# A product-key expert layer: the scores x·U of tiles 1 to 3 formed densely and stored beside a copy of V

## The chip, the cores and the metric

One core of a Trainium2 chip runs the whole program. The metric is the device time of one execution in microseconds, the median of three runs.

## What is computed

One layer of a hybrid decoder for 512 prompt tokens and 8 sample tokens: two token mixers, then an expert layer (PEER) and a last norm. The change lies in the expert layer. The reference, cut to it:

```python
# x: (T, 1024) after an RMSNorm; 16384 experts, each one row of u_tab and one of v_tab (1024 values)
q = einsum('td,de->te', x, w_q).reshape(T, 8, 2, 128)
s = einsum('thpd,hpkd->thpk', q, keys)                # 8 heads, 2 axes, 128 keys
s_top, i_top = top_k(s, 16)                           # on each axis
cand = s_top[:, :, 0, :, None] + s_top[:, :, 1, None, :]      # 256 pairs
best, sel = top_k(cand, 16);  eidx = i0 * 128 + i1 of sel     # expert numbers
gate = softmax(best)
act  = gelu(einsum('td,thkd->thk', x, u_tab[eidx]))   # x . U of the chosen experts
y    = einsum('thk,thkd->td', gate * act, v_tab[eidx])
```

Every token uses 8 x 16 = 128 experts. h + y, normalised, is the output.

## The kernel before

Tokens are cut into tiles of 128 (0 to 3) and a tile of 8 samples. Before the experts run the phases of the mixers: `small_projection`, `stream` (the big projections, weights streamed by SP's queue and split into an upper and a lower part, so that each product is three matmuls, `mm3`), `convolve`, `delta_solve`, `delta_finish`, `retention`. In `convolve` and `delta_solve` a helper `Side` computes other projections beside: SP loads a weight of 512 KB (`load`), ACT rounds it (`round`, L646), POOL forms the lower part (L620), PE multiplies, ACT takes the product (L663).

The last phase is `experts`. A *unit* u is one head of one tile: 32 units and one for the samples. A *slot* n is one of the 16 experts of a unit: 4 x 128 slots, and 8 more in which the samples' 1024 experts lie spread over the partitions, 520 in all. `order` is the order of slots, p a place in it.

- POOL, for each slot (L1954): an indirect DMA that fetches for each of the 128 tokens the row of its expert from `peer_uv`, U and V side by side, 2048 floats, into one of RING = 7 buffers `uv_row`.
- DVE (`dot`, L2228): the product of the U half with x, summed into a column of `coef` (which lies in `ret_tables`).
- ACT (`row`, L2077 to L2087): GELU, times the gate, and a diagonal 128x128 matrix `spread` with it.
- PE (`add_row`, L1995): `spread` times the V half into PSUM, in float32, two halves of 512 columns, four matmul records in the trace. For the few slots in `by_vector` DVE adds coef times V instead (`add_vector`, L2236). A buffer is free when that is done, and POOL waits for it (`row_used`).
- In between, after slots given by the tables QUERIES_AT, TAKES_AT, SPLITS_AT and UPPERS_AT: the query projections (PE `queries`, with weights split by ACT L2057 and DVE L2162), scores, and on DVE the four steps of `retrieve` (top 16 of both axes, of the 256 pairs, expert numbers) and `normalise`. Tile by tile `add`, `root` and `scale` make the output.

DVE's work at the start of the phase: `make_x` and `lower_x` (L2279) give x, its upper and its lower part for the five tiles.

## Time and profile before

| | us |
|---|---|
| median of 3 runs | 2221.38 |
| lowest, highest | 2214.74, 2225.39 |
| span of the profiled execution | 2217.6 |
| first gather issued | 852.6 |
| last gather issued | 2193.3 |

The windows view cuts the span into stretches: for each, how long every engine was busy, the clock that TensorE was granted (1.00 is full), the share of time in which the 16 DMA engines were busy, and what they moved. Such a row tells what ends last in a stretch. The list of instructions in order of time then gives the price of a single piece of work and the distance from one to the next, and a view by line gives shortest, median and longest duration. A matmul's recorded duration covers its way through the array, so the distance between two starts is its price. The seven buffers hold what has been fetched and not yet used: as long as POOL waits for one to come free, DMA has work queued.

### The profile page before, as it was taken

How to read it: one execution, taken by the hardware profiler on the slowest of the kernel's cores; microseconds unless marked ns; L12 is line 12 of the kernel's file. 1: busy time of each engine (PE TensorE's matmuls, PEld its weight loads, DVE VectorE, ACT ScalarE, POOL GpSimd, SP SyncE). 2: the span in 40 equal slices, each digit the busy share in tenths (PEclk: the TensorE clock that was granted, in tenths of full speed). 3: DMA queues.
4: the chain of work that ended last, by engine and by line, in shares of the span. 5: the costliest groups of instructions: out<-in, count | busy, mean ns of one | idle time of the engine just before them, and what ended most of it. 6: DMA issues, size and time to landing. Idle time of an engine off the chain costs nothing.

```text
span 2217.6 us, 25834 instructions
## 1 busy us (share of the span) xinstructions
PE 1812.9 (82%) x8648; PEld 1169.7 (53%) x8648; DVE 1313.7 (59%) x2828; ACT 872.2 (39%) x2271; POOL 632.8 (29%) x553
## 2 busy tenths in 40 slices
PE   5989889979987888898887777777777777777776
PEld 4988889969966887565532222222323322222222
DVE  3127353353363537677766766767667866766764
ACT  4223322242244324444434444444443444444443
POOL 0002012100000002454434444444344443444442
PEclk8999899979998998999999999999999999999999
DMA  3313122335015329999999999999999999999997
GB/s 115 123 44 94 29 58 72 99 104 180 22 65 192 115 76 367 334 413 416 395 393 419 420 419 420 420 420 418 393 420 409 419 418 419 402 420 420 419 415 301
DMA packets 171933, 637.36 MB, mean 287 GB/s; under 512 B 12546, under 2 KB 97605, under 8 KB 104856
## 3 DMA queue, kind: packets, MB, share of 16 engines
q0 software_dynamic: 74880, 545.29, 60.0%
q1 hardware_dynamic: 96928, 90.50, 12.9%
q8 instruction: 66, 1.08, 0.2%
q14 instruction: 59, 0.48, 0.1%
HBM read 617.92 MB, written 17.93 MB: 287 GB/s over the span
## 4 chain that ended last, share of the span: by engine, by line
DMA 31%; PE 13%; DVE 8%; ACT 8%; issue 3%; DVEq 0%; ACTq 0%
DMA ex_uv_row<-in_peer_uv,ex_eidx 31%; PE ps L1995 10%; DVE ex_uv_row L2228 5%; ACT ex_spread L2087 2%; ACT L2077 1%; ACT ret_tables L2082 1%; ACT L2071 1%; PE ps L570 1%; PE ps L572 1%; PE ps L571 1%; ACT ret_tables L2077 1%; DMA ex_uv_row<-in_peer_uv,ex_eidx_s 1%; DVE ex_fin L2236 0%; DVE ex_w_lo L2162 0%; DVE ex_top_i L2190 0%
## 5 line engine op out<-in xcount | busy, mean ns | idle before, releaser
L1995 PE MATMUL ps<-ex_uv_row,ex_spread 128*128 128x512 f32 (+1 forms) x2016 | 964.0, 612 | 278.8 <-ACT ex_spread L2087 278.3
L1954 POOL DMA_INDIRECT ex_uv_row<-in_peer_uv,ex_eidx x512 | 561.2, 1096 | 1004.6 <-PE ps L1995 716.3
L2228 DVE CUSTOM_DVE_ANT_0 ex_uv_row<-ex_uv_row,x_ffn 128x1024 f32<-128x1024 f32 x512 | 624.2, 1225 | 360.4 <-DMA ex_uv_row<-in_peer_uv,ex_eidx 356.1
L1995 PEld LDWEIGHTS ps<-ex_uv_row,ex_spread 128*128 128x128 f32 (+1 forms) x2016 | 351.0, 189 | 851.5 <-issue 851.3
L2077 ACT ACTIVATE ret_tables<-ret_tables 128x1 f32<-128x1 f32 x520 | 104.9, 202 | 644.8 <-DVE ret_tables L2228 643.4
L2087 ACT ACTIVATE ex_spread<-square,ret_tables 128x128 f32<-128x128 f32 (+1 forms) x504 | 201.5, 400 | 16.5
L2082 ACT ACTIVATE ret_tables<-ret_tables 128x1 f32<-128x1 f32 x512 | 150.6, 294 | 17.1 <-ACT ret_tables L2077 0.2
L570 PE MATMUL ps<-proj_b_whi,x_lo 128*128 128x256 f32 (+1 forms) x320 | 91.1, 285 | 7.4 <-DVE proj_b_wlo L479 7.0
L570 PE MATMUL ps<-x_hi,ex_w_lo 128*128 128x260 f32 (+1 forms) x272 | 90.7, 334 | 6.1 <-DVE x_lo L2279 3.1
L572 PE MATMUL ps<-proj_b_whi,x_hi 128*128 128x256 f32 (+1 forms) x320 | 90.6, 283 | 0.0
L571 PE MATMUL ps<-proj_b_wlo,x_hi 128*128 128x256 f32 (+1 forms) x320 | 90.6, 283 | 0.0
L620 POOL TENSOR_TENSOR dp_w_lo<-dp_w_raw,dp_w_hi 128x1024 fp32r<-128x1024 f32 x14 | 33.9, 2427 | 171.5 <-ACT dp_w_hi L646 171.5
L571 PE MATMUL ps<-x_lo,ex_w_hi 128*128 128x260 f32 (+1 forms) x272 | 79.1, 291 | 0.0
L572 PE MATMUL ps<-x_hi,ex_w_hi 128*128 128x260 f32 (+1 forms) x272 | 79.0, 290 | 0.0
L634 PE MATMUL ps<-x_hi,dp_w_lo 128*128 128x260 f32 x224 | 66.3, 296 | 0.0
L636 PE MATMUL ps<-x_hi,dp_w_hi 128*128 128x260 f32 x224 | 63.8, 285 | 0.0
L635 PE MATMUL ps<-x_lo,dp_w_hi 128*128 128x260 f32 x224 | 63.7, 284 | 0.0
L620 POOL TENSOR_TENSOR cv_w_lo<-cv_w_raw,cv_w_hi 128x1024 fp32r<-128x1024 f32 x8 | 20.5, 2562 | 151.3 <-ACT cv_w_hi L646 151.3
L570 PEld LDWEIGHTS ps<-x_hi,ex_w_lo 128*128 128x128 f32 x272 | 54.2, 199 | 13.4 <-issue 6.8
L570 PEld LDWEIGHTS ps<-proj_b_whi,x_lo 128*128 128x128 f32 (+1 forms) x320 | 55.0, 172 | 9.5 <-issue 7.1
L570 PE MATMUL ps<-x_hi,proj_a_wlo 128*128 128x260 f32 x192 | 55.3, 288 | 5.0 <-DVE proj_a_wlo L479 5.0
L1078 ACT ACTIVATE Y<-ps 128x512 f32<-128x512 f32 x24 | 14.4, 599 | 110.1 <-PE ps L1031 110.1
(408 smaller groups left out, 3234.5 us busy)
## 6 DMA issues: line engine op xcount, KB each, us to landing
first_raw<-in_w_in SPq DMA_DIRECT2D x8, 1024.0 KB, 8.6
ex_uv_row<-in_peer_uv,ex_eidx POOLq DMA_INDIRECT x512
dp_w_raw<-in_w_in SPq DMA_DIRECT2D x14, 512.0 KB, 4.1
proj_a_raw<-in_w_in SPq DMA_DIRECT2D x4, 1024.0 KB, 5.2
cv_w_raw<-in_w_in SPq DMA_DIRECT2D x8, 512.0 KB
proj_b_raw<-in_w_in SPq DMA_DIRECT2D x4, 1024.0 KB, 5.4
S_sample<-in_state_ret SPq DMA_DIRECT2D x1, 4096.0 KB, 22.3
out_ret_s<-S_sample SPq DMA_DIRECT2D x4, 1024.0 KB, 4.4
```

The costliest lines, as they stand in the source:

```text
L570: pe.matmul(out, left(llo, c), right(rhi, c), start=(c == 0), stop=False)
L571: pe.matmul(out, left(lhi, c), right(rlo, c), start=False, stop=False)
L572: ins = pe.matmul(out, left(lhi, c), right(rhi, c), start=False, stop=(c == kc - 1))
L634: pe.matmul(out, self.w_lo[n % 2][:, c, :], self.hi[:, c, ts], start=(c == 0), stop=False)
L635: pe.matmul(out, self.w_hi[n % 2][:, c, :], self.lo[:, c, ts], start=False, stop=False)
L636: ins = pe.matmul(out, self.w_hi[n % 2][:, c, :], self.hi[:, c, ts], start=False, stop=(c == DC - 1))
L1954: pool.indirect_dma_start(uv_row[:, p % RING, :], None, a["peer_uv"][0], bass.IndirectOffsetOnAxis(ap=index_of(n), axis=0)).then_inc(row_l ...
L1995: ins = pe.matmul(k.pv[j % 2][0:r, c, :], spread[:, p % RING, 0:r], uv_row[:, p % RING, D + c * 512:D + (c + 1) * 512], start=first, stop= ...
L2077: fence(act, act.activation(c, c, ACT.Gelu), weighed, 2 * p + 1)
L2082: fence(act, act.activation(c, c, ACT.Copy, scale=gate_of(n)), weighed, 2 * p + 2)
L2087: act.activation(spread[:, p % RING, 0:what.shape[1]], what, ACT.Copy, scale=c).then_inc(spread_done, 1)
L2228: dve.tensor_tensor_reduce(u, u, x, 1.0, 0.0, ALU.mult, ALU.add, coef[:, n:n + 1]).then_inc(dotted, 1)
```

## The change

The table of experts has 16384 rows, in 128 blocks of 128. For tiles 1 to 3, 384 tokens, the change computes gelu(x U) for *all* experts by matmul, block by block, and stores 384 values per expert in a new DRAM tensor `value_rows`, one row per expert of 128 + 1024 + 256 floats: the values of tile 1, V, those of tiles 2 and 3. A gather of such a row for a token brings V and, next to it, the 128 values of its tile, of which the token's own is picked by the identity matrix.

- V is copied into `value_rows` by 16 DMAs of 1024 rows each, from DRAM to DRAM, that ACT issues: 4 in `convolve`, 12 in `delta_solve`.
- U comes transposed by blocks (`peer_ut`, laid out by the host as `peer_uv` is) and is loaded block by block, 512 KB each, like the query weights, through three buffers (DEEP = 3) for raw, upper and lower part. The order of blocks is `expert_blocks`: 16 blocks of queries among 128 of activities. ACT rounds (`upper`), DVE and POOL take turns at the lower part (`lower`), PE multiplies (`activities`, 24 matmuls of 384 columns), ACT applies GELU from PSUM (`activate`), SP stores 512 and 1024 bytes a row (`store`).
- Tile 0 keeps its paired rows, one slot for each block of activities, three blocks behind (LAG); all of them are added by DVE. The samples' 8 paired slots follow.
- Then the 384 slots of tiles 1 to 3 gather 1152 or 1280 floats a row into 11 buffers that lie where `uv_row` was. DVE makes the diagonal matrix itself (`picked`, one operation of 128 columns), every fourth slot it adds alone; ACT has no part in a slot.
- x of tiles 1 to 4 is kept in the upper half of q until its transposes are made; tile 0's in `x_first`.

The core of the diff:

```diff
+    def copy_values(self, act):
+        n = self.copies
+        part = slice(n * NE // COPIES, (n + 1) * NE // COPIES)
+        act.dma_start(self.value_rows[part, P:P + D], self.peer_uv[part, D:2 * D]).then_inc(self.values_copied, 16)
+        self.copies = n + 1
...
@@ convolve, ACT
                     act.activation(pre[:, c, 0:NP_TOK], taps[:, c % 2, :], ACT.Silu).then_inc(silu_done, 1)
+                    if c % 3 == 0:
+                        k.copy_values(act)
@@ delta_solve, ACT
                         act.activation(Y[:, n % 2, :, :], bank(4 + n % 2), ACT.Copy).then_inc(y_done, 1)
+                        if n % 2 == 0:
+                            k.copy_values(act)
@@ experts, SP
+                def load(i):
+                    kind, n = blocks[i]
+                    if i >= DEEP:
+                        lowered(sp, i - DEEP)
+                    src = columns(a["peer_wq"][0], n * P, P) if kind == "q" else a["peer_ut"][n]
+                    sp.dma_start(w_raw[i % DEEP][:, :, :], src).then_inc(w_loaded[i % DEEP], 16)
+                def store(b):
+                    sp.wait_ge(z_made, b + 1)
+                    to = k.value_rows[b * P:(b + 1) * P, :]
+                    sp.dma_start(to[:, 0:P], z_rows[:, b % DEEP, 0:P]).then_inc(z_stored[b % DEEP], 16)
+                    sp.dma_start(to[:, P + D:WROW], z_rows[:, b % DEEP, P:BT]).then_inc(z_stored[b % DEEP], 16)
@@ experts, POOL
-                    row_used(pool, p)
-                    pool.indirect_dma_start(uv_row[:, p % RING, :], None, a["peer_uv"][0],
-                                            bass.IndirectOffsetOnAxis(ap=index_of(n), axis=0)).then_inc(row_loaded[p % RING], 16)
+                for i, (kind, n) in enumerate(blocks):
+                    if kind == "z" and AHEAD <= n - LAG + AHEAD < PAIRS and n >= LAG:
+                        gather_pair(n - LAG + AHEAD)
+                    if 5 <= i + 2 < len(blocks) and not by_dve(i + 2):
+                        lower(pool, i + 2)
...
+                pool.wait_ge(k.values_copied, 16 * COPIES)
+                pool.wait_ge(vector_done, HK)
+                pool.wait_ge(v_done, PER_ROW)
+                for b in range(DEEP):
+                    pool.wait_ge(z_stored[b], 32 * len(range(b, NE // P, DEEP)))
+                for p in range(PAIRS, SLOTS):
+                    gather_value(p)
@@ experts, PE
+                def activities(i, b):
+                    lowered(pe, i)
+                    wait(pe, z_made, b - 1)
+                    mm3(pe, k.pb[b % 2][:, 0:BT], DC, lambda x, c: x[:, c, :], w_hi[i % DEEP], w_lo[i % DEEP],
+                        lambda x, c: x[:, c, P:NP_TOK], x_hi, x_lo).then_inc(z_mm, 1)
@@ experts, ACT
+                def activate(b):
+                    act.wait_ge(z_mm, b + 1)
+                    wait(act, z_stored[b % DEEP], 32 * (b // DEEP))
+                    act.activation(z_rows[:, b % DEEP, :], k.pb[b % 2][:, 0:BT], ACT.Gelu).then_inc(z_made, 1)
...
+                for i, (kind, n) in enumerate(blocks):
+                    if i and blocks[i - 1][0] == "z":
+                        activate(blocks[i - 1][1])
...
+                    if i and i + 2 < len(blocks):
+                        upper(i + 2)
+                    if kind == "z" and n >= LAG:
+                        row(n - LAG)
@@ experts, DVE
+                def picked(p):
+                    n, m = order[p], p - PAIRS
+                    z = value_slot(p)[2]
+                    dve.wait_ge(gated, place[n // TOPK] + 1)
+                    dve.wait_ge(value_loaded[m % VALUES], 16 * (m // VALUES + 1))
+                    if p in by_vector:
+                        own.fence(dve.tensor_tensor_reduce(z, z, k.eye, gate_of(n), 0.0, ALU.mult, ALU.add, coef[:, n:n + 1]))
+                    else:
+                        wait(dve, v_done, on_tensor[p] - SPREADS + 1)
+                        dve.scalar_tensor_tensor(spread[:, on_tensor[p] % SPREADS, :], z, gate_of(n), k.eye,
+                                                 ALU.mult, ALU.mult).then_inc(diagonal, 1)
```

How it moves instructions. On ACT in `delta_solve`, before (Y is the Y of the solve, dp_result a product of the side work):

```order
L1078 ACTIVATE Y<-ps 128x512
L646 ACTIVATE dp_w_hi<-dp_w_raw 128x1024
L663 ACTIVATE dp_result<-ps 128x260
L1078 ACTIVATE Y<-ps 128x512
L663 ACTIVATE dp_result<-ps 128x260
```

and after:

```order
L1111 ACTIVATE Y<-ps 128x512
L177 DMA value_rows<-in_peer_uv 1024x1024
L656 ACTIVATE dp_w_hi<-dp_w_raw 128x1024
L673 ACTIVATE dp_result<-ps 128x260
L1111 ACTIVATE Y<-ps 128x512
L673 ACTIVATE dp_result<-ps 128x260
```

Behind every second Y stands the issue of a copy, ahead of the rounding. On DVE among tile 0's slots, before (L2228 is a dot, two rows each; L2208 to L2216 the last step of a retrieval):

```order
L2228 ISA ex_uv_row,ret_tables<-ex_uv_row,x_ffn 128x1024
L2228 ISA ret_tables 128x1
L2208 TENSOR_SCALAR ex_pick<-ex_sel 128x16
L2209 TENSOR_SCALAR ex_pick<-ex_sel 128x16
L2211 TENSOR_TENSOR ex_hot<-ex_pick,square 128x512
L2213 TENSOR_TENSOR ex_hot<-ex_hot,ex_top_f 128x512
L2215 TENSOR_REDUCE ex_res<-ex_hot 128x32
L2216 SCALAR_TENSOR_TENSOR ex_eidx<-ex_res 128x16
L2228 ISA ex_uv_row,ret_tables<-ex_uv_row,x_ffn 128x1024
L2228 ISA ret_tables 128x1
```

and after (L2367 dot, L2379 addition of V, L1929 lower part):

```order
L2367 ISA ex_uv_row,ret_tables<-ex_uv_row,x_first 128x1024
L2367 ISA ret_tables 128x1
L2379 SCALAR_TENSOR_TENSOR ex_fin<-ex_uv_row,ret_tables,ex_fin 128x1024
L1929 TENSOR_TENSOR ex_w_lo<-ex_w_raw,ex_w_hi 128x1024
L2367 ISA ex_uv_row,ret_tables<-ex_uv_row,x_first 128x1024
L2367 ISA ret_tables 128x1
L2379 SCALAR_TENSOR_TENSOR ex_fin<-ex_uv_row,ret_tables,ex_fin 128x1024
```

Each dot is now followed by the addition, and every second block by a lower part. On POOL, the whole phase before:

```order
L1954 DMA ex_uv_row<-in_peer_uv,ex_eidx 128x2048 x384
L1954 DMA ex_uv_row<-in_peer_uv,ex_eidx_s 128x2048 x8
L1954 DMA ex_uv_row<-in_peer_uv,ex_eidx 128x2048 x128
```

and after, the last rows of it:

```order
L2040 DMA ex_uv_row<-in_peer_uv,ex_eidx 128x2048 x2
L1929 TENSOR_TENSOR ex_w_lo<-ex_w_raw,ex_w_hi 128x1024
L2040 DMA ex_uv_row<-in_peer_uv,ex_eidx 128x2048
L2040 DMA ex_uv_row<-in_peer_uv,ex_eidx_s 128x2048 x8
L2051 DMA ex_uv_row<-value_rows,ex_eidx 128x1152 x256
L2051 DMA ex_uv_row<-value_rows,ex_eidx 128x1280 x128
```

Subtractions stand among the pairs' gathers, and the value gathers behind them all.

## Rows read from the trace of the kernel before

**Rows 1.** Windows: length, busy us (count) per engine, PE clock, DMA share, GB/s.

```profile
500.00:610.00 110.00, 108.31 (x921) 102.66 (x921) 40.00 (x47) 28.14 (x47) 1.42 (x2) 1.00 0.31 98
1100.00:1860.00 760.00, 584.48 (x1360) 230.48 (x1360) 528.02 (x1275) 333.43 (x984) 315.83 (x298) 0.99 1.01 415
```

**Rows 2.** The page: its span, and the chain that ended last.

```profile
span 2217.6 us, 25834 instructions
...
DMA 31%; PE 13%; DVE 8%; ACT 8%; issue 3%; DVEq 0%; ACTq 0%
```

**Rows 3.** By line, POOL's gathers: ns min/median/max, first and last start.

```profile
L1954 POOL DMA_INDIRECT ex_uv_row<-in_peer_uv,ex_eidx x512: 932/937/1988, 852.6 to 2193.3; - x171
```

**Rows 4.** In order of time: start, length, engine, line, [idle before it].

```profile
378.46 0.60 ACT L1078 ACTIVATE Y<-ps 128x512 f32<-128x512 f32 x1 [4.68 <-PE ps L1031]
...
380.69 0.43 SPq L600 DMA_DIRECT2D dp_w_raw<-in_w_in  x1
...
389.60 0.60 ACT L1078 ACTIVATE Y<-ps 128x512 f32<-128x512 f32 x1 [4.68 <-PE ps L1031]
...
390.09 1.05 ACT L646 ACTIVATE dp_w_hi<-dp_w_raw 128x1024 fp32r<-128x1024 f32 x1
...
395.17 0.60 ACT L1078 ACTIVATE Y<-ps 128x512 f32<-128x512 f32 x1 [3.75 <-PE ps L1031]
...
828.82 4.67 SPq L1905 DMA_DIRECT2D wq_raw<-in_peer_wq  x1
```

**Rows 5.** DMA issues, 300-432 and 1200-1700 us: KB each, us to landing.

```profile
dp_w_raw<-in_w_in SPq DMA_DIRECT2D x10, 512.0 KB, 4.1
...
out_y_p<-ex_fin SPq DMA_DIRECT2D x2, 512.0 KB, 8.2
```

**Rows 6.** In order of time, PE: the first and the last of 147 matmuls.

```profile
739.80 0.28 PE L571 MATMUL ps<-x_lo,branches_whi 128*128 128x260 f32 x1
...
757.22 0.28 PE L570 MATMUL ps<-x_hi,branches_wlo 128*128 128x260 f32 x1
```

**Rows 7.** The page's DMA queues: packets, MB, share of 16 engines over the span.

```profile
q0 software_dynamic: 74880, 545.29, 60.0%
q1 hardware_dynamic: 96928, 90.50, 12.9%
```

**Rows 8.** By line, DVE: dot, addition of V, lower part; ns min/median/max.

```profile
L2228 DVE CUSTOM_DVE_ANT_0 ex_uv_row<-ex_uv_row,x_ffn x512: 1205/1225/1301, 859.0 to 2206.1; 128x1024 f32<-128x1024 f32 x171
...
L2236 DVE SCALAR_TENSOR_TENSOR ex_fin<-ex_uv_row,ret_tables,ex_fin x16: 1278/1284/1285, 865.9 to 2209.3; 128x1024 f32<-128x1024 f32 x16
...
L2162 DVE TENSOR_TENSOR ex_w_lo<-wq_raw,ex_w_hi x8: 1215/1220/1221, 834.1 to 1101.6; 128x1024 fp32r<-128x1024 f32 x8
```

**Rows 9.** In order of time, DVE: last x_lo, two dots, the last dot.

```profile
856.11 1.36 DVE L2279 TENSOR_TENSOR x_lo<-ps,x_hi 128x1024 fp32r<-128x1024 f32 x2 [0.52 <-ACT x_hi L2110]
...
1516.22 1.22 DVE L2228 CUSTOM_DVE_ANT_0 ex_uv_row<-ex_uv_row,x_ffn 128x1024 f32<-128x1024 f32 x1
...
1517.40 1.23 DVE L2228 CUSTOM_DVE_ANT_0 ex_uv_row<-ex_uv_row,x_ffn 128x1024 f32<-128x1024 f32 x1
...
2206.13 1.23 DVE L2228 CUSTOM_DVE_ANT_0 ex_uv_row<-ex_uv_row,x_ffn 128x1024 f32<-128x1024 f32 x1 [1.25 <-DMA ex_uv_row<-in_peer_uv,ex_eidx]
```

**Rows 10.** In order of time, convolution: taps alone, and beside POOL's subtraction.

```profile
168.35 2.33 DVE L894 SCALAR_TENSOR_TENSOR conv_taps<-pre,vecs,conv_taps 128x512 f32<-128x512 f32 x3
...
179.25 4.35 DVE L894 SCALAR_TENSOR_TENSOR conv_taps<-pre,vecs,conv_taps 128x512 f32<-128x512 f32 x3
...
179.79 2.46 POOL L620 TENSOR_TENSOR cv_w_lo<-cv_w_raw,cv_w_hi 128x1024 fp32r<-128x1024 f32 x1 [3.64 <-ACT cv_w_hi L646]
```

**Rows 11.** In the chain of waits: twelve matmul records of three rows on PE.

```profile
943.51 5.15 PE ps L1995 x12
```

**Rows 12.** The page's group of the gathers: busy us, mean ns | idle before.

```profile
L1954 POOL DMA_INDIRECT ex_uv_row<-in_peer_uv,ex_eidx x512 | 561.2, 1096 | 1004.6 <-PE ps L1995 716.3
```

**Rows 13.** In order of time, POOL: a gather's issue, [idle before it].

```profile
854.00 0.94 POOL L1954 DMA_INDIRECT ex_uv_row<-in_peer_uv,ex_eidx  x1 [0.30 <-issue]
```

518 lines of the change are left out of this document (310 added, 208 removed).

## The prediction

> **What bounds the kernel now.** I read the windows by stage first, because the share of a whole span mixes stages. From 1100 to 1860 us the DMA share is 1.01 at 415 GB/s, while PE is busy 584 of 760 us, DVE 528 and ACT 333 [rows 1]. That is the stage that gathers one paired row (U and V, 8 KB for each of 128 partitions, 1.0486 MB) for each of 520 slots. The chain of waits agrees: its largest piece by far is the gather, 31% [rows 2]. 1.0486 MB at 415 GB/s is 2.53 us, and 520 gathers run from 852.6 to 2193.3 us [rows 3]. Before the gathers, from 500 to 610 us for example, DMA moves 98 GB/s and PE is busy 108 of 110 us [rows 1]: there the matmuls bound, and DMA is three quarters idle. The change attacks the bytes of the first stage and spends DMA in the second and matmuls in the first. So the question is what a "block" of the new dense stage costs, and what a slot of the new value stage costs.
>
> **What is there before the experts.** 16 copies of 4.19 MB, HBM to HBM, are issued by ACT: four in the convolution and twelve in the delta solve, one behind every second Y, whose period is 11.1 us (378.46 to 389.60) [rows 4]. No such copy is in the trace. Bounds: each byte once through the engines at 415 GB/s is 10.1 us a copy; each byte twice is 20.2. By the first all is done by about 432 us, by the second by about 560. Who can suffer: the side load behind which ACT waits. It is issued at 380.69, wanted at 390.09, lands in 4.1 us; beside saturated gathers a load or store of this size takes 8.2 [rows 4, 5], still under 9.4. And ACT itself: SP's fifth issue in a row took 4.67 us where a single one takes 0.4 [rows 4], so a queue with about four such transfers open holds its issuer. At 20.2 us a copy the twelfth finds 12 x (1 - 11.1/20.2) = 5.4 open; some 3 issues would be held for up to 9 us. ACT has 3.75 us of idle before each Y. Cost 0 to 27 us; I take 5, nearer to none because every named wait has slack.
>
> **The dense stage.** I count one unit: 16 blocks of activities and 2 of queries; there are eight (the last without queries, -11 us).
> - PE: 147 matmuls of 260 columns start between 739.80 and 757.22 us, 0.1193 us apart at full granted clock [rows 6]. 384 columns: 0.176 if all of it scales, 0.171 if only columns at 2.4 GHz are added. 16 x 24 x 0.171 = 65.7, queries 2 x 48 x 0.1193 = 11.5, scores about 0.6: **78 us** (80 by the upper price).
> - DMA: from the two queues of the page, 284 ns for 7282 bytes and 47 ns for 934 bytes an engine (share x span x 16 / packets), I work out 12.3 ns a packet plus 0.0373 ns a byte [rows 7]. 16 pairs x 2.53 = 40.4, 16 U blocks (8 packets of 4 KB an engine) x 1.32 = 21.1, two query weights 4.0, stores of z in 512 and 1024 byte runs 16 x 0.65 = 10.5: **76 us**.
> - DVE: dots follow each other at 1.18 us (1516.22 to 1517.40), the addition of V is 1.28: 16 x 2.46 = 39.4. Half of the lower parts, 9 x 1.22 = 11.0 [rows 8, 9]. Retrieval: 528.0 us busy less 304 dots of 1.30 is 132 us over 19 units, 6.9, with its gaps about 8; normalise 0.4. Sum 59.
> - On top, POOL takes the other 9 lower parts. What that does to DVE is in the convolution: three taps take 2.33 us alone and 4.35 with one POOL subtraction beside them, so DVE stands 2.0 us for each [rows 10]. 9 x 2.02 = 18. DVE with what it is made to wait: **77 us**. A gather's own issue stretches from 0.94 to at most 1.99 and does not stretch the dots (1301 ns at most) [rows 3, 8].
> - The three raw buffers: load 8.2 us under load, ACT's upper part 1.05, lower part 1.22 or 2.46 (on POOL), and about 2.5 behind the dot and the addition that stand ahead in DVE's order: 13 to 14.2 us for three blocks [rows 4, 5, 8, 10], 4.3 to 4.7 a block, 78 to 85 us a unit.
> ACT has about 2.4 us of work in 4.3. Four limits within ten per cent, coupled by in-order waits, do not reach the largest of them: I take 84 us a unit, the buffers' figure. 8 x 84 - 11 = **661 us**; ends 613 (PE alone) and 750 (95 a unit: POOL's 2.37 and its wait both added, and no overlap).
> The stage starts when the last x_lo is made. That was at 857.5 [rows 9]; a retrieval of 8 us that stood ahead now stands behind, so 852 is taken. End: 852 + 661 = 1513.
>
> **Between the stages.** Value rows lie where the pairs lay, so POOL waits for the last pair to be used. After the last block DVE has 11 dots, 5 additions, a retrieval and a normalise: 13 + 6.4 + 8.5 = 28, then ACT and PE 5: 33 us, in which six gathers (15 us) are hidden and DMA falls idle. 1546, first value row 3 us later.
>
> **The value stage.** 256 rows of 4608 and 128 of 5120 bytes a partition. By bytes at 415 GB/s 1.42 and 1.58 us; with the cost of a packet worked out above 1.48 and 1.63. The middle: 256 x 1.45 + 128 x 1.61 = **577 us** (566 to 588). Beside it: PE, 294 of 384 rows; a row of four matmul records costs 1.72 (5.15 for three) [rows 11], and 12 x 1.72 + 0.6 = 21.2 in a unit of 16 against DMA's 23.2. DVE about 19. POOL 0.94 for an issue, 1.10 on average as it waits for DVE, and 0.30 to the next: 1.40 a slot against 1.45 [rows 3, 12, 13]. All hidden, but POOL by 3% only.
> The end is as it was: the last dot starts at 2206.13, 11.5 us before the end of the span [rows 2, 9].
>
> **Sum.** 1546 + 3 + 577 + 11.5 + 5 (copies) = 2143 of span. The profiled execution has a span of 2217.6, and the median of the runs, 2221.4, lies 3.8 above it (runs from 2214.7 to 2225.4); the profile gives no time of its own outside the span. Forecast 2143 + 3 = **2146 us**, 3.4% faster. The gather stage gives 1353 up for 661 + 36 + 577.
>
> **Rivals.**
> A, slower: the raw buffers decide the dense stage and their loads land later than 8.2 us, since not only gathers but gathers and z stores stand ahead of them. Every microsecond of landing costs 144 / 3 = 48 us, because PE, DVE and the gathers all follow the blocks. It outweighs the gain from a landing of 9.8 us; at 11 the time is 2146 + 134 = 2280. For it: DMA is 76 of 84 us busy there, a share at which the only landings measured are already double. Against: the 8.2 was measured at a share of 1.0.
> B, copies at 20 us and ACT held at every issue from the first: 12 x 9.1 = 109 us, 2250. Against: four transfers fit before SP is held, and a third of that is nearer, 2175. The Trainium skill ("DMA: Bandwidth & Descriptors", Latency and other measured facts) gives 214 GB/s for a good copy between HBM tensors; by that a copy takes 19.6 us, an estimate, and the slow side of my bounds would hold: all copies done only by about 550 us, and 2175 rather than 2146. No row here shows a copy between HBM tensors of this size, so none confirms it.
> C, faster: DVE and POOL find each other's gaps and PE alone bounds at 78 us a unit: 613, and value rows cost bytes only, 566: 2087.
> D, POOL bounds the value stage: its wait for DVE grows since DVE's short operations come oftener; 1.55 a slot is 595, and with a unit at 90 us (+48) the time is 2212, no change.
> That the gather does not shrink is no rival: the shapes 128x1152 and 128x1280 stand in the program.
>
> **How the numbers follow.** Chance of the forecast and what lies around it (2105 to 2200) 0.56; C 0.14; the mild form of B is inside the first; D 0.10; A 0.14; strong B 0.06. A measurement of this kernel can tell 0.5%, 11 us, from no change. Faster by more (under 2210): 0.56 + 0.14 + 0.03 = 0.73; within 0.5%: 0.09; slower: 0.18. The range that leaves out 2 in 10: from C's 2087 to 2240, where the dense stage costs its upper end of 750 (2235).
>
> **What would show it.** Right: windows of the dense stage with DMA near 0.9, PE near 0.93 of the time, 4.6 us a block; lower parts on POOL of about 2.5 us and DVE additions that stand beside them; value stage at DMA 1.0, 1.45 to 1.6 us a gather; stages up to 825 us unmoved. Wrong: ACT's upper part waiting for the load (A); ACT's copy issues of many microseconds and later Y's (B); POOL without idle time among the value gathers (D). The working is wrong as a whole if a block takes over 5.1 us, for then nothing is gained.

## The result, and the profile after

The changed kernel takes 2280.2 us (median of 4 runs, 2274.0 to 2285.4), the kernel before 2218.3: a ratio of 1.027, 95% interval 1.024 to 1.030. It is slower by 2.7%, where 2146 us and 3.4% faster had been forecast, and outside the range of 2087 to 2240. The profiled execution has a span of 2283.6 us against 2217.6 [rows 2].

These are lines of the page of the changed kernel: the span, PE's granted clock and the DMA share in 40 slices of 57 us, the queues with packets, MB and share of the 16 engines, and the chain that ended last.

```profile
span 2283.6 us, 29645 instructions
...
PEclk9997788887799989999999999999999999999999
DMA  3316415988350154269999999999989999999997
...
q0 software_dynamic: 74880, 377.52, 42.0%
q1 hardware_dynamic: 152224, 182.80, 23.4%
q10 hardware_dynamic: 16640, 67.11, 8.6%
...
PE 24%; DMA 14%; DVE 11%; issue 5%; POOL 2%; ACT 1%; SPq 0%; DVEq 0%; another core or an unknown queue 0%; ACTq 0%; POOLq 0%
```

q0 and q1 answer to [rows 7]: the gathers move 377.5 MB where they moved 545.3. q10 is new, the sixteen copies of V. In the chain PE now has the largest share and no longer DMA as in [rows 2]; by line its largest piece is still a gather, that of the value rows, with 11% where the paired rows had 31%. In the slices from the fourth to the tenth the DMA share is up to 9 and PE's granted clock is down to 0.7; that is the convolution and the delta solve, where the copies run.

Two windows answer to [rows 1]: the dense stage from its first activity to its last, and the gathers of values (length, busy us and count for PE, PEld, DVE, ACT and POOL, clock, DMA share, GB/s).

```profile
998.90:1648.50 649.60, 627.19 (x3740) 621.57 (x3738) 572.85 (x762) 293.46 (x595) 363.89 (x196) 0.99 0.96 357
...
1677.80:2258.50 580.70, 521.41 (x1230) 220.27 (x1231) 420.11 (x1332) 21.40 (x62) 400.30 (x384) 1.00 1.01 406
```

In the first PE is busy 627.2 of 649.6 us. The forecast counted from the last x_lo, which is made by 977.0 here: on that measure the stage takes 671.5 us where 661 were forecast. The second has a DMA share of 1.01 at 406 GB/s, like the gathers of before.

By line, this is the row of the activities z on ACT (ns min/median/max, first and last start):

```profile
L2202 ACT ACTIVATE ex_z_rows<-ps x128: 491/493/496, 998.9 to 1648.5; 128x384 f32<-128x384 f32 x128
```

and of the gathers of values:

```profile
L2051 POOL DMA_INDIRECT ex_uv_row<-value_rows,ex_eidx x384: 935/941/2003, 1677.8 to 2258.5; - x192
```

128 activities from 998.9 to 1648.5 us. 384 gathers start between 1677.8 and 2258.5: 1.512 us each, where 1.45 and 1.61 (1.503 in the mean) were forecast. So the two new stages take nearly what was said. But both lie some 130 us late, since the dense stage can begin only when the mixers have ended. The place of the delay is in ACT's waits (us in total, times, longest):

```profile
ACT ex_w_hi L2189 <- DMA ex_w_raw<-in_peer_ut: 91.6, 46, 6.8
ACT cv_w_hi L656 <- DMA cv_w_raw<-in_w_in: 74.9, 6, 17.4
ACT dp_w_hi L656 <- DMA dp_w_raw<-in_w_in: 73.1, 5, 15.1
```

The last two are new in size (in the kernel before it is 10.6 us for cv_w_hi and nothing for dp_w_hi): 148 us in which ACT, whose work is in order, stands before the upper part of a side weight and waits for its load. In the convolution it looks like this, on ACT (start, length, engine, line, [idle before it and what ended it]):

```profile
174.41 0.61 ACTq L177 DMA_DIRECT2D value_rows<-in_peer_uv  x1
...
194.39 1.06 ACT L656 ACTIVATE cv_w_hi<-cv_w_raw 128x1024 fp32r<-128x1024 f32 x1 [16.42 <-DMA cv_w_raw<-in_w_in]
```

SP's load between them:

```profile
176.02 0.98 SPq L610 DMA_DIRECT2D cv_w_raw<-in_w_in  x1
```

ACT issues a copy at 174.41, SP a side load at 176.02, and ACT waits 16.42 us for it, until 194.39. In the kernel before the same load and the same use stood so, on SP:

```profile
174.38 0.44 SPq L600 DMA_DIRECT2D cv_w_raw<-in_w_in  x1
```

and ACT's use of it:

```profile
178.65 1.06 ACT L646 ACTIVATE cv_w_hi<-cv_w_raw 128x1024 fp32r<-128x1024 f32 x1 [2.31 <-DMA cv_w_raw<-in_w_in]
```

The load landed in 4.3 us, and ACT waited 2.31 us for it even then. This row was not among those the prediction rests on: in the convolution a side load had no slack at all, before any copy.

In the delta solve, a stretch of ACT in order of time that answers to [rows 4]:

```profile
395.55 0.50 ACTq L177 DMA_DIRECT2D value_rows<-in_peer_uv  x1
...
406.67 0.50 ACTq L177 DMA_DIRECT2D value_rows<-in_peer_uv  x1
...
421.64 1.06 ACT L656 ACTIVATE dp_w_hi<-dp_w_raw 128x1024 fp32r<-128x1024 f32 x1 [14.38 <-DMA dp_w_raw<-in_w_in]
```

and SP's load:

```profile
397.92 0.64 SPq L610 DMA_DIRECT2D dp_w_raw<-in_w_in  x1
```

The load that took 4.1 us [rows 5] takes 23.7, and the Y behind it waits. This is so for every second load of the solve: the one issued in between, at 388.17, finds the copies nearly done and is used at 396.18 without a wait.

### The profile page after: what moved, and what is told of

It reads as the page before. It is cut to its first block, busy times and chain, and to the rows that moved or that the text cites. A ratio compares the mean times of both kernels' runs of the same rounds, so it can differ in the third digit from the quotient of the medians.

```text
span 2283.6 us, 29645 instructions
## 1 busy us (share of the span) xinstructions
PE 1960.3 (86%) x10912; PEld 1591.0 (70%) x10912; DVE 1397.7 (61%) x2791; ACT 611.5 (27%) x1217; POOL 845.6 (37%) x625
## 4 chain that ended last, share of the span: by engine, by line
PE 24%; DMA 14%; DVE 11%; issue 5%; POOL 2%; ACT 1%; SPq 0%; DVEq 0%; another core or an unknown queue 0%; ACTq 0%; POOLq 0%
DMA ex_uv_row<-value_rows,ex_eidx 11%; PE ps L2129 9%; PE ps L580 5%; PE ps L582 5%; PE ps L581 5%; DVE ex_fin L2379 4%; DMA ex_w_raw<-in_peer_ut 3%; POOL ex_uv_row L2051 2%; DVE ex_uv_row L2367 2%; DVE ex_w_lo L1929 1%; ACT ex_w_hi L2189 0%; DVE ex_q_s L2392 0%; DMA ex_w_raw<-in_peer_wq 0%; DVE ex_hot L2349 0%; DVE ex_top_i L2326 0%
## 5 line engine op out<-in xcount | busy, mean ns | idle before, releaser
L2129 PE MATMUL ps<-ex_uv_row,ex_q_s 128*128 128x512 f32 (+1 forms) x1208 | 544.5, 600 | 76.2 <-DVE ex_q_s L2392 46.3
L2129 PEld LDWEIGHTS ps<-ex_uv_row,ex_q_s 128*128 128x128 f32 (+1 forms) x1208 | 216.9, 187 | 387.7 <-issue 357.1
L2051 POOL DMA_INDIRECT ex_uv_row<-value_rows,ex_eidx x384 | 401.2, 1045 | 195.3 <-issue 95.1
L580 PE MATMUL ps<-x_hi,ex_w_lo 128*128 128x384 f32 (+2 forms) x1296 | 428.0, 330 | 21.1 <-DVE ex_w_lo L1929 15.2
L582 PE MATMUL ps<-x_hi,ex_w_hi 128*128 128x384 f32 (+2 forms) x1296 | 425.0, 328 | 0.0
L581 PE MATMUL ps<-x_lo,ex_w_hi 128*128 128x384 f32 (+2 forms) x1296 | 424.6, 328 | 0.0
L2379 DVE SCALAR_TENSOR_TENSOR ex_fin<-ex_uv_row,ret_tables,ex_fin 128x1024 f32<-128x1024 f32 x218 | 364.2, 1671 | 15.0 <-ACT ret_tables L2219 14.9
L1929 POOL TENSOR_TENSOR ex_w_lo<-ex_w_raw,ex_w_hi 128x1024 fp32r<-128x1024 f32 x72 | 187.9, 2610 | 407.8 <-ACT ex_w_hi L2189 407.2
L581 PEld LDWEIGHTS ps<-x_lo,ex_w_hi 128*128 128x128 f32 x1296 | 245.8, 190 | 0.0
L582 PEld LDWEIGHTS ps<-x_hi,ex_w_hi 128*128 128x128 f32 x1296 | 245.6, 190 | 0.0
L2040 POOL DMA_INDIRECT ex_uv_row<-in_peer_uv,ex_eidx x128 | 183.6, 1434 | 116.3 <-DVE ex_fin L2379 98.7
L2367 DVE CUSTOM_DVE_ANT_0 ex_uv_row<-ex_uv_row,x_first 128x1024 f32<-128x1024 f32 x128 | 175.3, 1370 | 1.0
L1929 DVE TENSOR_TENSOR ex_w_lo<-ex_w_raw,ex_w_hi 128x1024 fp32r<-128x1024 f32 x72 | 88.5, 1229 | 68.0 <-ACT ex_w_hi L2189 49.0
L630 POOL TENSOR_TENSOR cv_w_lo<-cv_w_raw,cv_w_hi 128x1024 fp32r<-128x1024 f32 x8 | 20.2, 2534 | 205.2 <-ACT cv_w_hi L656 205.2
```

The lines of the kernel that those rows point to most:

```text
L580: pe.matmul(out, left(llo, c), right(rhi, c), start=(c == 0), stop=False)
L581: pe.matmul(out, left(lhi, c), right(rlo, c), start=False, stop=False)
L582: ins = pe.matmul(out, left(lhi, c), right(rhi, c), start=False, stop=(c == kc - 1))
L1929: eng.tensor_tensor(w_lo[b][:, :, :], w_raw[b][:, :, :], w_hi[b][:, :, :].bitcast(F32), ALU.subtract).then_inc(split_v if by_dve(i) else s ...
L2040: pool.indirect_dma_start(uv_row[:, p % RING, :], None, a["peer_uv"][0], bass.IndirectOffsetOnAxis(ap=index, axis=0)).then_inc(pair_loaded ...
L2051: pool.indirect_dma_start(value_slot(p)[0], None, k.value_rows, bass.IndirectOffsetOnAxis(ap=eidx[:, u, n % TOPK:n % TOPK + 1], axis=0), e ...
```

## Experiments: did the copies cost it, and where

All runs compare with the kernel before on the same chip (2215.3 to 2217.3 us in the four groups). The theory after the first look, called T: the copies cost nothing by themselves; side loads land late behind them and hold ACT, Y and PE. Rivals: another part of the change delays the mixers (R), or the new stages pay for the copies too (W).

**Without copies.** The value rows are gathered from the paired tensor with unchanged shapes, so that what is added is not V.

```
-                    if c % 3 == 0:
-                        k.copy_values(act)
...
-                        if n % 2 == 0:
-                            k.copy_values(act)
...
-                    pool.indirect_dma_start(value_slot(p)[0], None, k.value_rows,
+                    pool.indirect_dma_start(value_slot(p)[0], None, k.peer_uv,
...
-                pool.wait_ge(k.values_copied, 16 * COPIES)
```

> The changed kernel without the sixteen copies of V; its value rows are gathered with the same shapes from the paired tensor instead (the values taken are therefore not V, only the bytes and the instructions are the same). Theory T: the copies cost nothing in themselves, but the side loads (512 KB in packets of 512 bytes) land behind them, ACT waits for them and with it Y and PE; all 128 to 131 us by which the dense stage began later come from that. Then the stages up to 825 us stand where they stood before, the first dense block at about 853, and the time is 2280 - 129 = 2151 (2143 to 2160). Rival R: the mixers are late for another reason that the change brings (its code, its placement of buffers, a lower clock by itself): then 2250 or more. A third, W: the dense stage or the value stage also pays for the copies: under 2140.

2155.6 us, ratio 0.972 (0.969 to 0.975). T's number was 2151. The activities, by line:

```profile
L2196 ACT ACTIVATE ex_z_rows<-ps x128: 472/493/497, 868.4 to 1522.2; 128x384 f32<-128x384 f32 x128
```

The first is at 868.4, 130.5 us earlier than with copies, and the stage takes 653.8 us against 649.6. All of the loss, then, lies ahead of the dense stage, and none of it in the new stages. R and W fall.

**The copies alone, in the kernel before.**

```
+                    if c % 3 == 0:
+                        k.copy_values(act)
...
+                        if n % 2 == 0:
+                            k.copy_values(act)
```

> The kernel before with the same sixteen copies at the same places and nothing else of the change; nobody reads what they write. By T the mixers are delayed as in the changed kernel and the rest is as before: 2218 + 129 = 2347 (2335 to 2360). By R, where the delay came with something else of the change, 2218 to 2245. Where gathers of the paired rows hid part of it: between the two, which the first gather's start would show (T: 852.6 + 130 = 983).

2355.6 us, ratio 1.064 (1.062 to 1.065): 140 us more, 9 above the expected 2347. ACT's waits are those of the changed kernel, to a microsecond:

```profile
ACT cv_w_hi L655 <- DMA cv_w_raw<-in_w_in: 74.7, 6, 17.7
ACT dp_w_hi L655 <- DMA dp_w_raw<-in_w_in: 73.6, 5, 15.2
```

Its gathers, by line:

```profile
L1969 POOL DMA_INDIRECT ex_uv_row<-in_peer_uv,ex_eidx x512: 932/938/1977, 984.1 to 2323.8; - x171
```

The first gather starts at 984.1, where [rows 3] have 852.6: 131.5 us. In the profiled execution that is the whole cost: its span is 2348.1 us, 130.5 more than 2217.6. It was the fastest of the four, at 2350.0 us, so the rest of the 140 is the spread of the runs. Nothing of the dense stage is in this kernel, so the copies and their places are a sufficient cause.

## Experiments: how a copy holds up a load on another queue

A copy of 4.19 MB takes 12.3 us of all sixteen engines: q10's 8.6% of 2283.6 us over 16 copies, or 189 ns for each of its 64 packets of 4 KB an engine. That is near the fast side of the prediction's bounds, 10.1 to 20.2, and still the loads took 18 to 24 us. T1: packets of the two queues take turns, and a load of 64 short packets an engine (512 KB in runs of 512 bytes) and the store issued just ahead of it (8 more) wait for a long one at each turn. T2: a load is served when the copies issued before it have moved.

**Shorter packets for the copies.**

```
+        quarters = lambda x: x.rearrange("n (a b) -> a n b", b=D // 4)
-        act.dma_start(self.value_rows[part, P:P + D], self.peer_uv[part, D:2 * D])...
+        act.dma_start(quarters(self.value_rows[part, P:P + D]), quarters(self.peer_uv[part, D:2 * D]))...
```

> The changed kernel with each copy's rows of 4096 bytes cut into four packets of 1024 bytes, the same bytes, issues and places. Two theories on why a side load lands after 15 to 24 us beside a copy. T1, turns by packet: each of the load's 64 packets an engine waits for about one packet of the copy (189 ns for 4096 bytes on the page of the changed kernel, 64 x (189 + 47) = 15 us); with packets of 1024 bytes, some 55 to 65 ns, it is 64 x 110 ns = 7 us and 2 of latency, which is inside the 9.4 us of slack: the time is 2150 to 2175. T2, order: a load issued behind a copy lands when the copies issued before it have moved their bytes, whatever their packets: no change, 2270 to 2290, or worse if short packets move fewer bytes in the same time.

2644.8 us, ratio 1.195 (1.192 to 1.199), which neither theory had. On ACT:

```profile
174.81 1.23 ACTq L178 DMA_DIRECT2D value_rows<-in_peer_uv  x1
...
186.38 1.06 ACT L657 ACTIVATE cv_w_hi<-cv_w_raw 128x1024 fp32r<-128x1024 f32 x1 [8.00 <-DMA cv_w_raw<-in_w_in]
186.57 33.62 ACTq L178 DMA_DIRECT2D value_rows<-in_peer_uv  x1
...
220.31 1.06 ACT L657 ACTIVATE cv_w_hi<-cv_w_raw 128x1024 fp32r<-128x1024 f32 x1 [31.29 <-issue]
```

A window in which nothing but the second copy moves:

```profile
204.00:218.00 14.00, 0.00 (x0) 0.00 (x0) 0.00 (x0) 0.00 (x0) 0.00 (x0) 0.50 0.27 97
```

With four times the packets a copy of 4.19 MB becomes an issue of 32 to 40 us on ACT's queue in 14 of the 16 places (the first of the convolution took 1.23 us, the first of the solve 0.64), and the engines are nearly three quarters idle while it trickles at 97 GB/s. That is a new cost, not the one in question. The side load issued at 176.42 lands at 186.38, in 10 us, while the copy ahead of it still moves; T2 says no such thing, T1 does. But the engines are not full beside this load, so its 10 us are no measure of the turns.

**Long packets for the loads.** The side loads read a tensor in which a partition's 4096 bytes lie together, so that what is computed from them is not the layer's.

```
-                         columns(self.w, side_column(self.tiles[n]), P)).then_inc(self.loaded[n % 2], 16)
+                         self.k.wide[self.tiles[n]]).then_inc(self.loaded[n % 2], 16)
```

> The changed kernel, copies as they are, with one size changed: the side loads of 512 KB come from a tensor in which each partition's 4096 bytes lie together, so a load has 8 packets of 4 KB an engine in place of 64 of 512 bytes (the side weights are therefore other numbers, and all that is made of them is wrong; bytes, instructions and waits are the same). T1, one packet of the copy for each packet of the load: 8 x (189 + 189) = 3 us and 2 of latency, where the load of 64 packets took 17.8 us beside a copy (64 x 278 ns): ACT's waits for side loads in the convolution and the delta solve go from 148 us to under 20 and the time is 2150 to 2175. T3, the two queues share bytes, or a load waits for the copy ahead of it: a load of the same bytes lands when it did, 2265 to 2285.

2225.8 us, ratio 1.004 (1.003 to 1.006): 54 us come back, between the two expectations. The first side load behind a copy lands in 12.5 us (176.44 to 188.97), the one in the delta solve that is issued at 333.09 in 12.5 too. T1 gave 5 (7 with the store's packets counted), T2 the end of the copy, at about 188 and 345: here T2 looks right. It is not: by the trace's records of single packets the copy issued at 174.83 ended at 192.2, with 725 of its 1024 packets moved when the load had landed. The solve's side loads span 166.5 us against 148.4.

**Half the copy at the old places.** Sixteen copies of 2.1 MB by ACT, the other half of the bytes from SP at the ends of three projections.

```
-COPIES = 16
+COPIES = 32
+COPIES_IN = {"proj_a": 4, "proj_b": 7, "branches": 0, "w_out": 5}
...
+                for _ in range(COPIES_IN[name]):
+                    k.copy_values(sp)
```

> The changed kernel with each of ACT's sixteen copies at its old place and half its size, 2.1 MB; the other 16 x 2.1 MB go from SP at the ends of three projections (4, 7, 5), where they cost nothing by the kernel with all copies behind loads. How a side load of 512 KB, issued by SP 1 to 2 us behind a copy of ACT, is held up. T2, order at the engines: it lands when the copy issued before it has moved (4.19 MB take 12.3 us by the page, so 14.5 + 4 = 18 us in the changed kernel, 17.8 measured; with wide packets 12.5 measured, though they were 8 in place of 64). Half the copy is 6.2 us: the load lands in 10 to 12 us. It costs then (10.5 - 4.1) / (17.8 - 4.1) of 59 us in the convolution, 27, and 2 us for each of some ten loads in the delta solve: 2150 + 47 = 2197 (2175 to 2215). T1, turns packet by packet: the copy still has 128 packets an engine for the load's 64, so every turn is taken as before, the load lands in 17 to 18 us, and only the second copy in the delta solve's 24 us falls away: convolution as late as in the changed kernel, 2225 to 2275.

2175.8 us, ratio 0.982 (0.980 to 0.984), at the lower edge of what T2 was given. On ACT:

```profile
174.98 0.61 ACTq L178 DMA_DIRECT2D value_rows<-in_peer_uv  x1
...
187.34 1.06 ACT L659 ACTIVATE cv_w_hi<-cv_w_raw 128x1024 fp32r<-128x1024 f32 x1 [8.81 <-DMA cv_w_raw<-in_w_in]
```

and SP's load:

```profile
176.59 0.84 SPq L613 DMA_DIRECT2D cv_w_raw<-in_w_in  x1
```

The load of 176.59 lands at 187.34, in 10.75 us. The first side load of the delta solve is at 283.1 us, against 255.6 in a kernel whose convolution has no copies (below): 27.5, where 27 was expected. The 20 us expected in the delta solve did not come: its loads land after 8.5 to 10.8 us, ACT waits 0.3 to 1.5 us each, and they span 150.5 us. There the 9.4 us of [rows 4] and ACT's own idle time do hold. But the reckoning of T1 in this expectation was wrong: 2.1 MB are 32 packets an engine, not 128, so the copy is used up before the load's turns are, and both theories give about 11 us.

**The same halves, issued behind the load.**

```
-                        if n % 2 == 0:
+                        if n % 2 == 1:
```

> The same with one place changed: in the delta solve the twelve copies of 2.1 MB stand behind the odd Ys in place of the even ones, so that ACT issues each 2 to 4 us behind a side load in place of 1 to 2 us ahead of it. T2: what is issued later does not hold a load up, the copy has moved within 6.2 us of an interval of 11.1, and the delta solve is as without copies (149 us from its first side load to its last), while the convolution costs what it costs in the kernel with half copies: 20 us less than that, 2177 (2160 to 2195). If the two kernels take the same time, the place in the order is not what counts and the solve pays for the bytes in flight as such.

2179.8 us, ratio 0.985 (0.982 to 0.987), not the 20 us less that were expected, for the reason just told: half copies had cost the solve nothing at the old place either. ACT's upper parts there have no wait at all now, where they had up to 1.5 us.

**Double copies.** The test that tells the theories apart is a copy that outlives the load.

```
-COPIES = 16
+COPIES = 8
...
-                    if c % 3 == 0:
+                    if c % 6 == 0:
...
-                        if n % 2 == 0:
+                        if n % 4 == 0:
```

> The changed kernel with eight copies of 8.4 MB in place of sixteen of 4.19 MB, each at the place of every second one. The kernel with half copies was reckoned wrongly: a copy of 2.1 MB has 32 packets of 4 KB an engine, not 128 (512 rows over 16 engines), fewer than the load's 64, so that by turns too the load outlives the copy and lands after 2 + 6.2 + what is left of its own, as measured: it did not tell T1 from T2. A copy longer than the load does. First side load behind a copy in the convolution, issued 1.6 us behind it. T1, turns: a load and the store ahead of it have 72 packets an engine, the copy 128, so 72 x (189 + 47) ns = 17 us and 2 of latency, 18 to 20 us, no more than the 17.8 beside 4.19 MB. T2, the copy ahead first: 2 + 24.6 + 4.3 - 1.6 = 29 us. The time tells less, since half of the loads have no new copy ahead: 2240 to 2290 by T1, 2270 to 2320 by T2.

> The same with side loads of long packets, 8 of 4 KB an engine and 8 of the store ahead of them (the side weights are other numbers, and what is made of them is wrong). T1, one packet of the copy for each: 16 x 189 + 2 of their own + 2 of latency = 7 us, and not the 11 to 12.5 measured beside 4.19 MB. T2: 2 + 24.6 + 0.5 - 1.6 = 25 us. T3, a fixed backlog: the engines have taken in some 8 to 10 us of the copy's packets before they see the load, and serve it then, however long the copy is: 11 to 12.5 us as beside 4.19 MB, and about 19 to 24 in the kernel with short packets.

The first takes 2270.5 us (ratio 1.025, 1.021 to 1.029), the second 2220.5 (1.002, 0.999 to 1.004); the first of these both theories allow. The loads with short packets, on ACT:

```profile
175.16 0.61 ACTq L177 DMA_DIRECT2D value_rows<-in_peer_uv  x1
...
201.71 1.06 ACT L656 ACTIVATE cv_w_hi<-cv_w_raw 128x1024 fp32r<-128x1024 f32 x1 [22.99 <-DMA cv_w_raw<-in_w_in]
```

and on SP:

```profile
176.78 0.88 SPq L610 DMA_DIRECT2D cv_w_raw<-in_w_in  x1
```

The load of 176.78 lands after 24.9 us: neither 19 (T1) nor 29 (T2). With long packets, on SP and then on ACT:

```profile
174.27 0.86 SPq L610 DMA_DIRECT2D cv_w_raw<-in_peer_ut  x1
...
188.88 0.42 SPq L610 DMA_DIRECT2D cv_w_raw<-in_peer_ut  x1
```

```profile
172.66 0.61 ACTq L177 DMA_DIRECT2D value_rows<-in_peer_uv  x1
...
187.15 1.06 ACT L656 ACTIVATE cv_w_hi<-cv_w_raw 128x1024 fp32r<-128x1024 f32 x1 [10.93 <-DMA cv_w_raw<-in_peer_ut]
...
200.36 1.06 ACT L656 ACTIVATE cv_w_hi<-cv_w_raw 128x1024 fp32r<-128x1024 f32 x1 [10.56 <-DMA cv_w_raw<-in_peer_ut]
```

The copy of 172.66 moves until about 207 us, as the GB/s of windows of 2 us show. Of the two loads issued while it moves the first lands in 12.9 us (174.27 to 187.15) and the second in 11.5 (188.88 to 200.36). The second is the clearest reading of the study: it was issued 16 us into a copy that had some 18 us still to go and landed before its end, in the time that its like took beside a copy half as long. T2 falls. T3 as the last expectation has it, the fixed backlog, stands in its main point: some of the copy's packets are ahead, an amount that does not grow with the copy, and from there on the queues take turns. Its size by sums: 16 turns of long packets are 16 x 189 + 2 us of their own + 2 of latency, 7 us, and 11.5 to 12.9 were measured; 72 turns of 236 ns and 2 are 19, and 24.9 were measured. Both leave 4.5 to 6 us, 24 to 31 packets of 189 ns.

The trace's records of single packets show both parts. Turns: in the kernel with short packets 541 packets of the copy and 544 of the load move between 188 and 195 us, one for one. Backlog: the first packet of SP's queue, one of the store ahead of the load, moves 0.45 us after the load's issue where no copy is in flight. Beside long packets of a copy it moves 4.7 us after the issue at 176.78, and 3.4 us after the one at 188.88; meanwhile 16 and 19 packets an engine of the copy go ahead. From issue to landing the copy moves 104 packets an engine beside the load with short packets, where turns alone make 72, and 42 and 47 beside those with long ones, where turns make 16: 26 to 32 more each time. So half of the excess or somewhat more stands ahead of SP's first packet; the rest comes later, before the slowest of the sixteen engines is done. What holds SP's first packet back is not shown.

In the changed kernel's delta solve, where the second copy of a pair is issued before the first is done, the same excess gives 19 + 5.5 = 24.5, and 23.7 and 24.4 were measured; in the convolution the single copy ends first, and 18.4 us is the moving of both. The kernel with short packets for the copies is not explained: there SP's first packet moves 0.46 us after the issue, as with no copy, and 72 turns of 93 ns (46 for a packet of the copy, 47 for one of the load) and 2 us are 8.7, where 10.0 were measured with engines that are mostly idle.

## Experiments: giving the copies another place

**In holes, from ACT.** 64 copies of 1 MB, in runs of up to 12, where no wanted load is in flight.

```
+COPIES_IN = {"proj_a": 8, "proj_b": 12, "branches": 6, "w_out": 8}
...
+                                    if after is None:
+                                        k.copy_values(act, COPIES_IN[name])
...
+                k.copy_values(act, 12)
```

> The changed kernel with the same bytes copied as 64 copies of 1 MB, and issued by ACT where no wanted load is in flight: 8 at the end of the first projection, 12 behind the convolution's side loads, 4 in the outputs of the delta layer, 12 at the end of the second projection, 14 in the retention, 6 at the end of the branches, 8 at the end of the output projection. By T (under T1 and under T2 alike) nearly all of the 129 us come back: 2151 and up to 10 for loads at the phases' starts, 2150 to 2165, which is faster than the kernel before. If the bandwidth itself was short, or ACT is held by a full queue at a run of 8 to 12 issues, it stays over 2200: L177 issues of several us in the trace of ACT would show the latter.

2231.0 us, ratio 1.007 (1.005 to 1.009). The forecast failed by the way named in its last sentence. On ACT, behind the convolution's side work:

```profile
224.66 23.58 ACTq L178 DMA_DIRECT2D value_rows<-in_peer_uv  x12
248.29 1.17 ACT L960 ACTIVATE l_sq<-pre 128x520 f32<-128x520 f32 x2 [23.25 <-issue]
```

Twelve issues take 23.6 us: ACT is held at the issue, and the squares of the norm behind it begin that much later. This is what the prediction's rival B feared, and it needs more in flight than the changed kernel has, whose sixteen issues took 0.50 to 0.61 us each. The run of eleven at the end of the second projection takes 22.7 us in the same way. The dense stage's first activity is at 939.7, 71 us later than without copies; the two runs are 46 of them, and the rest was not traced.

While ACT is held, nothing but copies moves:

```profile
236.00:246.00 10.00, 0.00 (x0) 0.00 (x0) 0.00 (x0) 0.00 (x0) 0.00 (x0) 0.50 0.96 321
```

**Behind the loads, from SP.** 64 copies of 1 MB again, on the queue of the loads, each behind the last load that is wanted soon.

```
             self.load(sp, n + 2)
+            if self.name == "dp" and 1 <= n + 1 <= 11:
+                self.k.copy_values(sp, COPIES_IN["dp"])
             sp.wait_ge(self.taken, 2 * n + 2)
...
                 side.on_sync(sp, tails_out)
+                k.copy_values(sp, COPIES_IN["cv"])
```

> The changed kernel with its copies cut into 64 of 1 MB, and all of them issued by SP on the queue of the loads, each behind a load: 10 at the end of the first projection, 11 behind the convolution's side work, 2 behind each of eleven side loads of the delta solve (period 11.1 us: load 4 us, then 2 x 3.1 of copies), 12 and 9 at the ends of two later projections. Theory T1 (packets of two queues take turns, packets of one queue go in order): a wanted load never has a copy's packet ahead of it, and a held issuer holds nobody, so the mixers are as without copies: 2156 and up to 8 for small stores that do wait, 2152 to 2165, faster than the kernel before. Rival H (the memory itself is what a copy takes from a load, or PE and DVE run slower beside one): the 60 us that the copies in holes on ACT still cost (2217.5 of span against 2157.1) stay in part: 2180 to 2230.

2149.8 us, ratio 0.970 (0.967 to 0.972): faster than the kernel before by 3.0%, and within 6 us of the kernel without copies, which it equals but for noise. On SP, in the delta solve:

```profile
353.02 0.43 SPq L613 DMA_DIRECT2D dp_w_raw<-in_w_in  x1
353.50 1.36 SPq L178 DMA_DIRECT2D value_rows<-in_peer_uv  x2
...
364.16 0.43 SPq L613 DMA_DIRECT2D dp_w_raw<-in_w_in  x1
```

The whole stretch from 300 to 420 us:

```profile
300.00:420.00 120.00, 119.20 (x1002) 118.96 (x1001) 46.90 (x72) 28.79 (x53) 24.46 (x11) 0.97 0.72 224
```

The activities' rows:

```profile
L2204 ACT ACTIVATE ex_z_rows<-ps x128: 490/491/495, 869.9 to 1513.3; 128x384 f32<-128x384 f32 x128
```

Every 11.1 us there is a load, and two copies behind it; DMA has a share of 0.72 in the solve and PE is busy 119.2 of 120 us. The activities of the dense stage begin at 869.9 and end at 1513.3, and the prediction's end of that stage was 1513.

Three things differ from the changed kernel: the size of a copy, its queue and its place. Which of them does it was not taken apart for the whole. In the delta solve alone, copies of 2.1 MB on ACT's own queue cost nothing either, at the old place (150.5 us from its first side load to its last) and behind the load (151.0), against 151.0 without copies.

**Lower parts on DVE only.** The same kernel with one more edit, in the dense stage.

```
-            return i < 2 or (i % 2 == 1 and i >= 5)
+            return i < 2 or i >= 5
```

> As the kernel with copies behind the loads, and one part of the dense stage changed: from the sixth block on all lower parts are made by DVE, none by POOL. The prediction put 18 us a unit on DVE because POOL's subtraction and DVE's operations stand in each other's way (2.0 us for each of nine), and got 77 for DVE against 78 for PE. Without them DVE has 39.4 + 22 + 8.3 = 70 and POOL's gathers stretch less. By that reading the dense stage is 0 to 3 per cent shorter: 2140 to 2160 against 2156 or what the kernel with copies behind the loads takes. Rival: the order on DVE decides, for a lower part must stand behind a dot and an addition of 2.5 us, PE waits more for its weights, and the stage is longer by up to 0.5 us a block: 2170 to 2230.

2135.8 us, ratio 0.964 (0.962 to 0.966): the fastest of all. Groups of instructions from 870 to 1497 us (busy us, mean ns, idle before), first with POOL's share of the lower parts:

```profile
L2381 DVE SCALAR_TENSOR_TENSOR ex_fin<-ex_uv_row,ret_tables,ex_fin 128x1024 f32<-128x1024 f32 x121 | 242.8, 2007 | 9.8 <-ACT ret_tables L2221 9.7
...
L1931 POOL TENSOR_TENSOR ex_w_lo<-ex_w_raw,ex_w_hi 128x1024 fp32r<-128x1024 f32 x69 | 183.1, 2654 | 146.4 <-ACT ex_w_hi L2191 146.1
...
L2369 DVE CUSTOM_DVE_ANT_0 ex_uv_row<-ex_uv_row,x_first 128x1024 f32<-128x1024 f32 x122 | 171.2, 1403 | 1.0
```

and without:

```profile
L1931 DVE TENSOR_TENSOR ex_w_lo<-ex_w_raw,ex_w_hi 128x1024 fp32r<-128x1024 f32 x138 | 168.6, 1223 | 94.3 <-ACT ex_w_hi L2191 92.9 <-DVE ex_eidx L2354 0.3
L2381 DVE SCALAR_TENSOR_TENSOR ex_fin<-ex_uv_row,ret_tables,ex_fin 128x1024 f32<-128x1024 f32 x125 | 160.0, 1280 | 0.0
L2369 DVE CUSTOM_DVE_ANT_0 ex_uv_row<-ex_uv_row,x_first 128x1024 f32<-128x1024 f32 x126 | 153.5, 1218 | 0.0
...
L2191 ACT ACTIVATE ex_w_hi<-ex_w_raw 128x1024 fp32r<-128x1024 f32 x138 | 146.1, 1059 | 173.0 <-DMA ex_w_raw<-in_peer_ut 123.5 <-DMA ex_w_raw<-in_peer_wq 49.3
```

The addition of V takes 1280 ns where it took 2007, the dot 1218 where it took 1403. Beside POOL's 69 subtractions DVE lost 121 x 0.727 + 122 x 0.185 = 110 us, 1.6 us for each; the prediction had 2.0. The Trainium skill ("SBUF — State Buffer", SBUF: two separate sides) says that a VectorE operation with two SBUF inputs and a GpSimd operation that reads SBUF exclude each other for a whole instruction; this pair of runs agrees. The stage gains 16 us of these 110: it goes from 643.4 to 627.6 us (869.7 to 1497.3), 4.36 us a block, PE busy 620. ACT waits longer for loads (173 us against 86), but PE is idle for only 7 us of 628: PE bounds the stage now.

## Why the prediction was wrong

**The copies: the step that failed.** It reads: "Who can suffer: the side load behind which ACT waits. It is issued at 380.69, wanted at 390.09, lands in 4.1 us; beside saturated gathers a load or store of this size takes 8.2 [rows 4, 5], still under 9.4", and "Cost 0 to 27 us; I take 5, nearer to none because every named wait has slack." The cost was 130. Two things were wrong in it.

- The landing. 8.2 us was measured for two stores in runs of 4096 bytes beside gathers, and for no load. The side load has 64 short packets an engine, and beside a copy each of them waits for one of 189 ns, with a backlog of some 30 on top: 18 to 24 us. Twice the price of bytes was the wrong law; it goes by the number of packets of the load and the length of the copy's. The price of a copy itself was right, near the low bound.
- The slack. It was read at one place, in the delta solve. In the convolution ACT waited 2.31 us for the load already. First side load of the delta solve, with and without copies: 309.8 against 254.6, 55 us, for four copies. From there to its last: 220 us against 148.4, 72 us, for twelve. 55 + 72 = 127 of the 130.

The bounds of this term had been taken from ACT's time at the issue alone, and so the range could not reach the result either. (The issue of 4.67 us from which they came is by the trace the sixth of its row, not the fifth.)

**The stages up to the experts unmoved.** Wrong by the same step. Where the copies stand behind the loads it is right: the dense stage's first activity comes at 869.9, with no copies at all at 868.4.

**The dense stage.** "I take 84 us a unit", 661 in all, from the last x_lo at 852 to 1513. On that measure it took 671.5 us in the changed kernel (977.0 to 1648.5) and 665.2 with copies behind the loads (848.1 to 1513.3). The size was right, the reason only in part: it was put on the three buffers, with PE alone at 613 and busy 0.93 of the time. PE was busy 649 of 671.5 us, 0.97, and the DMA share was 0.94. PE alone is no 613: its matmuls of 384 columns start 0.175 us apart (0.171 were taken), and all eight units have queries (11 us were taken off for the last). In the last kernel, from 847.8 to 1497.3, PE is busy 642 of 649.5 us. The 2.0 us that DVE stands for each of POOL's subtractions was 1.6; that this coupling costs time is shown by the 16 us that this kernel gains.

**Between the stages.** 36 us were forecast from the last block to the first gather of values; it was 29.3 from the last activity to it.

**The value stage.** 577 against 580.7 us. POOL's issue did not bound it (rival D): DMA's share is 1.01.

**The end.** 11.5 us were taken, from the last dot on. But the value stage was counted by the gathers' issues, and the way from the last issue to the last dot (2193.3 to 2206.13 before [rows 3, 9]) was put at nothing: 25 us lie between the last gather's issue and the end of the span, as 24 did before. With the 1.5 us of the last gather inside the 577, this term was some 12 us too small.

**The rivals.** B named the right culprit and the wrong mechanism: ACT was to be held at its issue, and its issues took half a microsecond. Its price for the strong form, 109 us, was near by accident, and it had 0.06. A was about late loads too, but in the dense stage, where ACT waited 92 us in 46 pieces and PE was busy nonetheless. Where the copies cost next to nothing the sum of 2146 holds to 4 us, at 2149.8, and that is luck in part: in its profile the end is 13.7 us longer than the sum has it, the dense stage 4.2 and the value stage 3.2, and against them stand 6.7 us between the stages, 3.9 of an earlier start and the 5 for the copies.

**The clock.** PE's granted clock in the mixers fell with the copies: between 170 and 590 us its mean over windows of 60 us is 0.68 to 0.88, a mix of 1.2 and 2.4 GHz, where PE stood waiting for up to 26 of the 60 us. It follows the waits: in the kernel with the same bytes behind the loads PE is busy 119.2 of 120 us from 300 to 420, and the granted clock is 0.97. Some of the 130 us may come by way of it, for the solve's side matmuls are busy 209 us where they were 194 before; its share was not measured apart.

## What to carry to other kernels

Before a bulk transfer is put beside latency-bound work, list every load that an in-order engine waits for while it runs, read the slack of each in each stage, and price a load by its packets: one packet of the other queue for each of its own, and a backlog ahead. The mean DMA share does not tell it. What worked here: small pieces on the queue of the wanted loads, each piece behind a load and done before the next. A queue of its own protects nobody: a load on another queue still takes turns with it. In the delta solve halves that were used up before the load's turns were did no harm on a queue of their own either, so the length of the piece may count for more than the queue; that was not tested for the whole kernel. An engine that computes should issue no long run of such pieces: it is held at the issue, and an idle issuer that is held holds nobody.
